# A hybrid attention layer on one core: gate and branch products for branch A first, then for branch B, with the first gates inside the last attention pair

## The reference, cut to what matters

```
h = rms_norm(x, g_pre_mix) * (1.0 + scale_m) + shift_m
proj = h @ w_in            # q, k, v of A and B, the forget logits, gate_logit (2 x 1024 columns)
o_a = sliding_window_gqa_sinks(...)     # (S, 512)
o_b = forgetting_attention(...)         # (S, 512): causal, 8 heads
gates = sigmoid(gate_logit).reshape(B, S, 2, D)
merged = gates[:, :, 0] * (o_a @ w_branch_a) + gates[:, :, 1] * (o_b @ w_branch_b)
y = merged @ w_out
x = x + gate_m * rms_norm(y, g_post_mix)
h = rms_norm(x, g_pre_ffn) * (1.0 + scale_f) + shift_f
x = x + gate_f * rms_norm((silu(h @ w_g) * (h @ w_u)) @ w_ffn_out, g_post_ffn)
```

## Time and profile before

| | us |
|---|---|
| median of 3 runs | 1658.65 (1655.44 to 1660.12) |
| the profiled execution, its own time | 1662.93 |
| its span, first to last instruction | 1661.1 |
| PE busy | 1522.7 (92%) |
| DVE busy | 606.9 (37%) |
| POOL busy | 603.1 (36%) |
| ACT busy | 418.4 (25%) |
| share of PE in the chain that ended last | 76% |

### The profile page before, as it was taken

The page is one execution under the profiler, slowest core; times in us unless marked ns, Lnnn a source line. Parts: engine busy times, 40 slices in busy tenths (PEclk is TensorE's granted clock), DMA queues, the critical chain, the costliest instruction groups (busy, mean ns, idle before and its releaser), DMA issues.

```text
span 1661.1 us, 19144 instructions
## 1 busy us (share of the span) xinstructions
PE 1522.7 (92%) x7273; PEld 1239.1 (75%) x7273; DVE 606.9 (37%) x930; ACT 418.4 (25%) x835; POOL 603.1 (36%) x519
## 2 busy tenths in 40 slices
PE   1599979799886899999899999999999999999998
PEld 1488756677665688888768788888888888788886
DVE  4673776655554576566556300000000000002002
ACT  2512056554543210100144300000000000333321
POOL 0501743332413133333112333332333332884860
PEclk9999999899997999999999999999999999999999
DMA  7400021111003534343223221111111111433431
GB/s 287 145 13 0 27 64 36 29 46 51 33 14 88 173 94 126 89 123 104 90 88 135 71 61 51 38 50 51 51 51 44 44 51 38 172 119 127 167 100 51
DMA packets 149674, 132.51 MB, mean 80 GB/s; under 512 B 13200, under 2 KB 130024, under 8 KB 149104
## 3 DMA queue, kind: packets, MB, share of 16 engines
q1 hardware_dynamic: 142960, 123.34, 23.7%
q10 hardware_dynamic: 6656, 8.39, 1.4%
HBM read 119.10 MB, written 12.62 MB: 79 GB/s over the span
## 4 chain that ended last, share of the span: by engine, by line
PE 76%; DVE 11%; ACT 5%; DMA 3%; issue 3%; POOL 2%; SPq 0%; ACTq 0%; DVEq 0%; POOLq 0%
PE PS L1285 64%; PE PS L1361 4%; PE PS L1415 2%; PE PS L1440 1%; DVE s_row L1050 1%; PE PS L1467 1%; POOL s_row L588 1%; ACT p_a L715 1%; PE PS L1468 1%; DMA xin<-in_x_dram 1%; DMA woraw<-in_w_out_dram 1%; DVE mx L1031 1%; ACT pt_hi L731 1%; PE PS L1296 1%; DVE rope_b L1000 1%
## 5 line engine op out<-in xcount | busy, mean ns | idle before, releaser
L1285 PE MATMUL PS<-act_hi,w_hi 128*128 128x512 f32 x960 | 375.4, 391 | 1.9 <-DVE ostage L1080 1.9
L1285 PE MATMUL PS<-act_hi,w_lo 128*128 128x512 f32 x960 | 374.2, 390 | 0.0
L1285 PE MATMUL PS<-act_lo,w_hi 128*128 128x512 f32 x960 | 374.1, 390 | 0.0
L1285 PEld LDWEIGHTS PS<-act_hi,w_hi 128*128 128x128 f32 x960 | 180.5, 188 | 39.2 <-issue 2.0
L1285 PEld LDWEIGHTS PS<-act_hi,w_lo 128*128 128x128 f32 x960 | 180.6, 188 | 37.9
L1285 PEld LDWEIGHTS PS<-act_lo,w_hi 128*128 128x128 f32 x960 | 180.7, 188 | 37.2
L550 POOL TENSOR_TENSOR scratch<-ones 128x1 f32<-128x1 f32 x68 | 13.4, 197 | 528.7 <-PE PS L1285 462.6
L559 POOL TENSOR_TENSOR w_lo<-wraw,w_hi 128x1024 fp32r<-128x1024 f32 x81 | 202.4, 2498 | 6.5
L1261 DVE TENSOR_TENSOR act_ff<-PS,sl 128x512 f32 x40 | 27.7, 692 | 407.6 <-PE PS L1285 407.6
L1285 PE MATMUL PS<-w_hi,ah_hi 128*128 128x512 f32 x352 | 137.0, 389 | 2.2 <-POOL w_lo L649 2.2
L1285 PE MATMUL PS<-w_lo,ah_hi 128*128 128x512 f32 x352 | 136.9, 389 | 0.0
(11 more groups left out here) (217 smaller groups left out, 2524.3 us busy)
## 6 DMA issues: line engine op xcount, KB each, us to landing
wraw<-in_w_ffn_in_dram SPq DMA_DIRECT2D x44, 512.0 KB
w2raw<-in_w_ffn_out_dram SPq DMA_DIRECT2D x44, 512.0 KB, 3.4
adaraw<-in_w_ada_dram SPq DMA_DIRECT2D x32, 512.0 KB, 4.0
wraw<-in_w_in_dram SPq DMA_DIRECT2D x25, 512.0 KB
wada<-in_w_ada_dram SPq DMA_DIRECT2D x4, 2048.0 KB, 9.7
xin<-in_x_dram SPq DMA_DIRECT2D x8, 512.0 KB, 10.2
cs<-ncum_dram SPq DMA_DIRECT2D x4, 1024.0 KB, 4.6
merged<-oT_dram ACTq DMA_DIRECT2D x8, 512.0 KB, 7.2
```

The costliest lines, as they stand in the source:

```text
L1285: ins = nc.tensor.matmul(out_ap, lhs[a], rhs[b], start=first and i == 0, stop=last and i == 2)
```

## The change

The rounds are ordered otherwise and written out, not looped. A round q is now 256 columns of one branch: q = 0 to 3 is branch A, q = 4 to 7 branch B; its two gate units are the two times 128 columns. So branch A's product goes into `merged` (72 KB on) alone, and rounds 4 to 7 add to it. The raw outputs of A (`oa_raw`) are loaded in pair 2 and split by POOL in pair 3; those of B are loaded behind the attention and split by POOL in rounds 0 to 3. The gates of round 0 are the chunks 26 to 29, put into the steps of pair 3. The ada blocks go 2, 4, 5, 5, 4, 4, 4, 4 to the rounds, with six buffers for their sums (two before). Rows 0 to 3 of w_out are loaded and split in rounds 4 to 7 (hi by ACT, lo by POOL, `wo_early`), rows 4 to 7 behind the last branch block. PE takes the three token blocks in the order 0, 2, 1. Some buffers moved with it.

```
     N_ROPE = 10
-    last_chunk = {n: max(j for j, c in enumerate(chunks) if c[0] == n) for n in range(13)}
+    N_PROJ = len(chunks)
+    chunks += [(13, 0), (13, 1), (14, 0), (14, 1)]
+    last_chunk = {n: max(j for j, c in enumerate(chunks) if c[0] == n) for n in range(15)}
...
+    for nth, (start, steps, gap) in enumerate(((0, 6, 6), (6, 6, 12), (12, 6, 18), (19, 5, 24))):
+        fills[N_PROJ + nth] = ([step0(B_P - 1) + start + i for i in range(steps)], step0(B_P - 1) + gap)
...
-    for n in range(7, 13):
+    for n in range(7, 16):
         split_at[fills[last_chunk[n - 2]][1]].append(n)
+    oa_step = {step0(B_P - 1) + k: f for f, k in enumerate((7, 9, 11, 14))}
+    ADA_Q = (2, 4, 5, 5, 4, 4, 4, 4)
+
+    def ada_blocks(q):
+        return range(sum(ADA_Q[:q]), sum(ADA_Q[:q + 1]))
+
+    def gates_of(q):
+        return 4 * (q - 1)
...
+            load_gate_unit(13)
+            load_gate_unit(14)
             load_forget(3)
+            sp.wait_ge(s_ready, N_S - NTOK)
+            for i in range(2):
+                sp.wait_ge(o_out[i], 16 * (A_T // 2))
+            for f in range(4):
+                sp.dma_start(oa_raw[:, f], oT_dram[f]).then_inc(oa_in, 16)
+            load_gate_unit(15)
             sp.wait_ge(grp_ready, step0(3) + 8)
...
+            load_ada(0)
+            load_ada(1)
+            load_gate_unit(16)
+            load_gate_unit(17)
+            sp.wait_ge(pv_done, NG)
+            for i in range(2):
+                sp.wait_ge(o_out[i], 16 * 12)
+            for f in range(4):
+                sp.dma_start(ob_raw[:, f], oT_dram[4 + f]).then_inc(ob_in, 16)
+            for q in range(8):
+                new = [a + 2 for a in ada_blocks(q) if a + 2 < N_ADA]
+                if q == 4:
+                    load_wo(0)
+                    load_wo(1)
+                if 0 < q < 7:
+                    load_gate_unit(16 + 3 * q)
+                for a in new[:3]:
+                    load_ada(a)
+                if 0 < q < 7:
+                    load_gate_unit(17 + 3 * q)
+                for a in new[3:]:
+                    load_ada(a)
+                if q < 7:
+                    load_gate_unit(18 + 3 * q)
+                if q > 5:
+                    load_wo(q - 4)
+            load_wo(4)
+            load_wo(5)
             for n in (N_FF, N_FF + 1):
                 sp.wait_ge(w_split, n - 1)
                 col = (n - N_FF) * DFF
                 sp.dma_start(wraw[:, n % 2], w_fi_v[:, :, col:col + P]).then_inc(w_in_s[n % 2], UNIT)
-            sp.wait_ge(m_split, 2 * KD)
+            load_wo(6)
+            load_wo(7)
+            sp.wait_ge(wo_split, 4)
             for t in range(2):
                 sp.dma_start(xr[:, t], x_v[t]).then_inc(xr_in[t], 16)
...
+            def split_outputs(f, raw, hl, loaded, hi_ok, split):
+                pool.wait_ge(loaded, 16 * 4)
+                pool.tensor_copy(hl[0][:, f], raw[:, f]).then_inc(hi_ok, 1)
+                pool.wait_ge(hi_ok, f + 1)
+                pool.tensor_tensor(hl[1][:, f], raw[:, f], hl[0][:, f].bitcast(F32), ALU.subtract).then_inc(split, 1)
...
+                if gp in oa_step:
+                    pool.wait_ge(s_ready, N_S)
+                    split_outputs(oa_step[gp], oa_raw, oa_hl, oa_in, oa_hi_ok, oa_split)
+
+            for n in range(16, N_FF):
+                split_att(n)
+                if n in (17, 20, 23, 25):
+                    split_outputs((17, 20, 23, 25).index(n), ob_raw, ob_hl, ob_in, ob_hi_ok, ob_split)
+                if n in (28, 31, 34, 36):
+                    k = (28, 31, 34, 36).index(n)
+                    pool.wait_ge(wo_hi_ok, k + 1)
+                    pool.tensor_tensor(wo_hl[k][1][:, :], woraw[:, k % 2], wo_hl[k][0][:, :].bitcast(F32), ALU.subtract)\
+                        .then_inc(wo_early, 1)
...
+                    if j >= N_PROJ:
+                        act.wait_ge(proj_ready, j + 1)
+                        act.wait_ge(s_taken, N_S)
+                        nc.scalar.activation(sg[:, j - N_PROJ], PS[:, chunk_bank(j)], ACT.Sigmoid).then_inc(g_done, 1)
...
-            act.wait_ge(pv_done, NG)
-            for i in range(2):
-                act.wait_ge(o_out[i], 16 * 12)
-            for p in range(8):
-                act.dma_start(merged[:, p, :], oT_dram[p]).then_inc(ob_in, 16)
...
+            for q in range(1, 8):
+                for j in range(4):
+                    gate(q, j)
+                if q == 4:
+                    act.wait_ge(br_ready, 16)
+                if q >= 4:
+                    wo_hi(q - 4)
+            for k in range(6):
                 merged_hi(k, 0)
+            act.wait_ge(br_ready, 32)
+            wo_hi(4)
+            merged_hi(6, 0)
+            wo_hi(5)
+            merged_hi(7, 0)
+            wo_hi(6)
+            wo_hi(7)
...
+            def branch_out(q, j):
+                k, cols = 2 * (q % 4) + j // 2, slice((j % 2) * NT, (j % 2 + 1) * NT)
+                dve.wait_ge(g_done, 4 * q + j + 1)
+                dve.wait_ge(br_ready, 4 * q + j + 1)
+                if q < 4:
+                    nc.vector.tensor_tensor(merged[:, k, cols], PS[:, BR_BANK[j]], sg[:, j], ALU.mult).then_inc(br_taken, 1)
+                else:
+                    nc.vector.tensor_tensor(sg[:, j], PS[:, BR_BANK[j]], sg[:, j], ALU.mult).then_inc(br_taken, 1)
+                    dve.wait_ge(br_taken, 4 * q + j + 1)
+                    nc.vector.tensor_tensor(merged[:, k, cols], merged[:, k, cols], sg[:, j], ALU.add).then_inc(merged_ok, 1)
...
+            for j in range(4):
+                branch_out(0, j)
+            for q in range(8):
+                for a in ada_blocks(q):
+                    ada_block(a)
+                if q == 7:
+                    for k in range(4):
+                        merged_lo(k, 0)
+                if q > 0:
+                    for j in range(4):
+                        branch_out(q, j)
+            wo_lo(4)
+            merged_lo(4, 0)
+            merged_lo(5, 0)
+            wo_lo(5)
+            merged_lo(6, 0)
+            wo_lo(6)
+            merged_lo(7, 0)
+            wo_lo(7)
...
+            def branch(q):
+                n = N_ATT + 3 * q + 2
+                pe.wait_ge(w_split, n + 1)
+                pe.wait_ge(oa_split if q < 4 else ob_split, 4)
+                if q == 0:
+                    pe.wait_ge(proj_taken, N_PROJ)
+                    pe.wait_ge(s_taken, N_S)
+                    pe.wait_ge(o_taken, len(o_step))
+                    pe.wait_ge(grp_lo, NG)
+                for j in range(4):
+                    if j == 3:
+                        pe.wait_ge(g_done, 4 * q + 4)
+                    elif q > 0:
+                        pe.wait_ge(br_taken, 4 * (q - 1) + j + 1)
+                    for kk in range(4):
+                        ins = product(PS[:, BR_BANK[j]], [w[:, n % 2, 2 * kk + j // 2] for w in w_hl],
+                                      [o[:, kk, (j % 2) * NT:(j % 2 + 1) * NT] for o in (oa_hl if q < 4 else ob_hl)],
+                                      kk == 0, kk == 3)
+                    ins.then_inc(br_ready, 1)
...
+            for q in range(8):
+                if q > 0:
+                    gates(q)
+                branch(q)
+                if q > 0:
+                    for a in (*(ada_blocks(0) if q == 1 else ()), *ada_blocks(q)):
+                        ada_sum(a)
...
-                pe.wait_ge(wo_split, k + 1)
+                pe.wait_ge(*((wo_early, k + 1) if k < 4 else (wo_split, k - 3)))
                 pe.wait_ge(m_split, k + 1)
-                for t in range(3):
+                for t in (0, 2, 1):
+                    if k == 0 and t > 0:
+                        pe.wait_ge(br_taken, 30 if t == 2 else 32)
```

More of the change, by code:

```diff
@@ L464, in _, with load_gate_unit @@
-            for k in range(KD):
-                if k >= 2:
-                    sp.wait_ge(wo_split, k - 1)
-                sp.dma_start(woraw[:, k % 2], w_out_v[k]).then_inc(wo_in[k % 2], 16)
+            def load_gate_unit(n):
+                q, r = divmod(n - N_ATT, 3)
+                slot, col = n % 2, (q % 4) * 2 * P
+                sp.wait_ge(w_split, n - 1)
+                if r < 2:
+                    c0 = C_G + (q // 4) * D + col + r * P
+                    sp.dma_start(wraw[:, slot], w_in_v[:, :, c0:c0 + P]).then_inc(w_in_s[slot], UNIT)
+                elif q < 4:
+                    for f in range(2):
+                        sp.dma_start(wraw[f * HD:(f + 1) * HD, slot].rearrange("p (g m) n -> p g (m n)", m=2),
+                                     w_a_v[f, :, :, col:col + 2 * P]).then_inc(w_in_s[slot], 16 + 16 * f)
+                else:
+                    sp.dma_start(wraw[:, slot].rearrange("p (g m) n -> p g (m n)", m=2), w_b_v[:, :, col:col + 2 * P])\
+                        .then_inc(w_in_s[slot], UNIT)
@@ L605, in _ @@
                     split_att(n)
-            pool.wait_ge(proj_ready, len(chunks))
-            with pool.Fori(0, KD // 2) as it:
```

(51 more changed lines are left out.)

164 lines of the change are left out of this document (55 added, 109 removed).

## The result

| | before | after |
|---|---|---|
| median of the runs, us | 1659.24 (1655.44 to 1660.12, 4 runs) | 1621.13 (1620.60 to 1622.68, 4 runs) |
| the profiled execution | 1662.93 | 1621.15 |
| its span | 1661.1 | 1619.4 |
| PE busy | 1522.7 (92%) | 1505.1 (93%) |
| POOL busy | 603.1 (36%) | 640.2 (40%) |

The ratio on record is 0.9755, with a 95% interval of 0.9736 to 0.9773. By the medians of the table it is 38 us faster (0.977), by the profiled executions 41.8. The forecast was 1616, with a range of 1609 to 1635.

What follows compares the result with a forecast made beforehand. PE was taken to bound the kernel (76% of the chain, busy 92%), so only its rests pay. Terms 4.7 + 0.5 - 32.6 - 0.7 - 2.4 - 12.2 = -42.7 us: 1662.93 to 1620.2, less 4.3 for the median: 1616, range 1609 to 1635.

Steps and rivals of the forecast that it cites:

- step 1: Pair 3 of the attention: 96 gate matmuls put into its rests cost +4.7 us, the sigmoid's table load +0.5.
- step 2: Behind the attention: the first branch block comes at once, -32.6 us, and regains half its low-clock loss, -0.7 us.
- step 3: The seven rounds behind the first branch block: two stops for ada sums become one of about 0.34 us, -2.4 us.
- step 4: Output product up to the third `grow`: w_out rows and merged split early let PE go on without rest, -12.2 us.
- the fill in series: Pair 3: the gate matmuls push each link of the chain instead of filling rests, 17.1 us more, 1633; chance 0.12.
- the output product still paced by others: Output product: loads of rows 6 and 7 or `diag` keep about 7 of the 12.2 us, 1623; chance 0.12.
- POOL holding up the weights: Rounds: an item waiting in POOL's queue delays weights beyond 6.5 us to spare, 48 us more, 1664; chance 0.02.

Runs made afterwards that it cites:

- the delayed kernels: Changed kernel with 8 or 16 extra POOL copies before the split of the first gate unit in rounds 2 to 7: 1625.15 and 1663.85 us.

## Why the prediction was right, and where it was not

Against the profiled execution the sum was -42.7 us, and -41.8 came. Term by term, predicted and measured:

| | predicted | measured |
|---|---|---|
| step 1, fill and table load | +4.7 + 0.5 | +4.8 |
| step 2, up to the first branch block | -32.6 | -32.7 |
| step 2, clock of that block | -0.7 | -1.6 |
| step 3, rounds | -2.4 | +0.4 |
| step 4, output product | -12.2 | -12.6 |
| start, and behind the third `grow` | 0 | -0.7 + 0.7 |

- **Step 1** held. The nearest row, pair 2, gave 4.7, and the experiment with the gates behind the attention shows 4.7 the other way (a repetition of the same kernel moved pair 3 by 0.8). The table load costs 0, not 0.5: POOL's wait covers it.
- **Step 2** held in size: the wait for the last copy of bank 6 stayed, the rest went. Its reason was incomplete: the 9.86 us are the last of eight loads, which took 13.1 together, and the last 6.9 us before the branch block were the wait for the ada sums, which the prediction names but doesn't price. The first branch block takes 43.78 - 32.81 = 11.0 us, the full clock from the start, not half of the gain: 1.6 us of rest behind a filled pair left the clock alone.
- **Step 3** failed. The step said that two stops of 0.34 us become one of the same length. The cost goes by sums, some 0.2 us each, and 32 of them stand in the seven rounds where 28 stood: 1.23 + 2 x 1.01 + 4 x 0.79 = 6.4 us against 7 x 0.68 = 4.8, +1.6; the products gave 1.2 back, 32.81 us a round where they were 21.93 + 11.05. A round is 33.6 us (four sums) to 34.0 (six), not 33.3, and the term is +0.4 where -2.4 was forecast. The row had the count (x4) beside the 0.34, and I did not ask what it scaled with.
- **Step 4** was right in size, with half the mechanism. Some 7.3 us are the early rows and `merged`, which no run takes apart; 4.7 are the end of a collision between POOL's split and `diag`, which lay in the 44.0 us as read and so came into the difference unseen. I looked for this collision in the changed kernel (`diag` near 19 instead of 16; it was made at 16.7) and not in the kernel before, where it was.
- **From the profiled execution to the median.** The forecast took 4.3 us off because the profiled execution of before lay that much above the median of three runs. After the change the profiled execution lies on the median, 1621.15 and 1621.13, 1621.61 and 1622.88 when run again, and the kernel before had medians of 1661.65, 1663.70 and 1662.48 over 7 to 15 later runs on two chips. That speaks for three low runs rather than a high profiled one; it isn't shown for those runs themselves. This step is 4.3 of the 5.1 us by which 1616 was low; the sum is the other 0.9. In the sum, step 3's 2.8 us were made up by smaller errors the other way, in the clock of the first branch block (0.9), in steps 1 and 4 (0.4 each) and elsewhere: that it came within 0.9 us was in part luck.

The rivals: the fill in series is refuted by experiment; the output product still paced by others has no rest to show for it; POOL holding up the weights does not occur, but its threshold of 6.5 us agrees with the delayed kernels.

## What to carry to other kernels

Price work that moves into a stage by a neighbouring stage that already carries as much, and count twice what it gives: it finds cover, and it keeps the clock up where the stage rested. Before the difference of two stages' lengths is called the gain of an edit, look in the old stage for instructions that take three times their usual length: such a collision may go, stay or move with a load's place in a queue, and it is no part of the edit. Before the time of a row is carried over to another number of stops, ask what it scales with. A correction from one profiled execution to the median of three runs is not worth making when the runs spread as widely as the correction.

## What the runs showed of the hardware

- A rest of 3.4 to 5.0 us in a full stage cost half as much again: 7 to 13 matmuls at 0.43 us (the lower of the two clock levels, 1.2 GHz) behind it, 1.5 to 2.7 us each time. A rest of 1.6 us behind a filled pair cost none.
- The hold-up between DVE and POOL works both ways: DVE's four `diag` instructions 3.69 us beside POOL's split and 0.88 alone; POOL's instruction on 128 x 1 elements 4.73 us beside DVE's eight lo halves, and 0.2 alone. The rule that the prediction cited from the Trainium skill (SBUF — State Buffer, SBUF: two separate sides) locks the pair of ports for the whole instruction, and the `diag` row agrees with it. The other goes further: POOL waited through all eight of DVE's instructions, not one.
- A row of attention outputs of 512 KB took 1.6 to 1.9 us when several were under way: eight landed within 13.1 us of the first issue, four within 7.5. The time from issue to landing of the last one alone, 9.86 and 6.17, holds its place behind the others.
- Stages that no edit touched differed by up to 3 us between executions in the part before pair 3, and by up to 4 in the tail, so an edit of 2 us is seen between landmarks and not in the median.
